# Latent attention of a two-block layer stack: a TensorE step begins with its scores, and each item's transposes stand ahead of another item's values

## The reference, cut to what matters

```
sc = jnp.einsum('bqhd,bkhd->bhqk', qi, k, preferred_element_type=jnp.float32) * scale
mask = key_chunk[None, :] <= q_chunk[:, None]
p = jax.nn.softmax(jnp.where(mask, sc, -jnp.inf), axis=-1)
return jnp.einsum('bhqk,bkhd->bqhd', p.astype(v.dtype), v)
```

## Time and profile before

| | us |
|---|---|
| median of 3 runs (2577.3 to 2577.61) | 2577.58 |
| the profiled execution | 2577.62 |
| its span in the trace | 2575.8 |
| PE busy in the span | 2557.3 |
| DVE busy | 1662.4 |
| ACT busy | 1276.7 |
| POOL busy | 360.7 |

### The profile page before, as it was taken

The page is one execution under the profiler, slowest core; times in us unless marked ns, Lnnn a source line. Parts: engine busy times, 40 slices in busy tenths (PEclk is TensorE's granted clock), DMA queues, the critical chain, the costliest instruction groups (busy, mean ns, idle before and its releaser), DMA issues.

```text
span 2575.8 us, 35285 instructions
## 1 busy us (share of the span) xinstructions
PE 2557.3 (99%) x12630; PEld 2030.0 (79%) x12630; DVE 1662.4 (65%) x2398; ACT 1276.7 (50%) x2142; POOL 360.7 (14%) x270
## 2 busy tenths in 40 slices
PE   9999999999999999999999999999999999999999
PEld 7855788888777557888888775799988777899887
DVE  4476677643988895677653778597633546687533
ACT  4326543333546895444333578577533425567432
POOL 0020100000103782100000130000610002000800
PEclk9999999999999999999999999999999999999999
DMA  5330232223243442233222230232232221232222
GB/s 216 106 94 21 91 107 97 92 97 98 82 133 123 131 131 81 72 109 98 96 93 96 95 103 10 65 116 101 89 112 93 96 97 51 97 123 99 82 98 98
DMA packets 74833, 250.44 MB, mean 97 GB/s; under 512 B 8764, under 2 KB 9148, under 8 KB 74336
## 3 DMA queue, kind: packets, MB, share of 16 engines
q1 hardware_dynamic: 73632, 240.63, 28.5%
q0 software_dynamic: 944, 8.33, 0.9%
q10 hardware_dynamic: 144, 0.00, 0.0%
HBM read 242.50 MB, written 2.24 MB: 95 GB/s over the span
## 4 chain that ended last, share of the span: by engine, by line
PE 92%; DVE 3%; ACT 2%; issue 1%; DMA 1%; SPq 0%; POOL 0%; DVEq 0%; ACTq 0%; POOLq 0%
PE bank L432 25%; PE bank L433 24%; PE bank L434 24%; PE bank L1361 2%; PE bank L1363 2%; PE bank L1362 2%; PE bank L2257 2%; PE bank L2808 1%; PE bank L654 1%; PE bank L639 1%; PE bank L3156 1%; PE bank L1706 1%; PE bank L640 1%; PE bank L1695 1%; PE bank L2264 1%
## 5 line engine op out<-in xcount | busy, mean ns | idle before, releaser
L383 DVE TENSOR_TENSOR wlo<-wraw,whi 128x1024 fp32r<-128x1024 f32 x344 | 441.5, 1285 | 448.8 <-ACT whi L360 448.2
L360 ACT ACTIVATE whi<-wraw 128x1024 fp32r<-128x1024 f32 x348 | 366.9, 1056 | 508.5 <-DMA wraw<-in_w 508.3
L432 PE MATMUL bank<-hnhi,whi 128*128 128x512 f32 (+1 forms) x1528 | 596.7, 390 | 1.1 <-DVE wlo L383 0.7
L433 PE MATMUL bank<-hnlo,whi 128*128 128x512 f32 (+1 forms) x1528 | 584.5, 383 | 0.0
L434 PE MATMUL bank<-hnhi,wlo 128*128 128x512 f32 x1392 | 542.1, 389 | 0.0
L432 PE MATMUL bank<-ahi,whi 128*128 128x512 f32 x1184 | 463.5, 391 | 1.9 <-DVE alo L712 1.1
L434 PE MATMUL bank<-ahi,wlo 128*128 128x512 f32 x1184 | 460.8, 389 | 0.0
L433 PE MATMUL bank<-alo,whi 128*128 128x512 f32 x1184 | 460.8, 389 | 0.0
L432 PEld LDWEIGHTS bank<-hnhi,whi 128*128 128x128 f32 x1528 | 287.2, 188 | 86.3 <-issue 29.5
L433 PEld LDWEIGHTS bank<-hnlo,whi 128*128 128x128 f32 x1528 | 287.4, 188 | 57.5 <-issue 3.4
L434 PEld LDWEIGHTS bank<-hnhi,wlo 128*128 128x128 f32 x1392 | 261.3, 188 | 55.7
(11 more groups left out here) (360 smaller groups left out, 3940.5 us busy)
## 6 DMA issues: line engine op xcount, KB each, us to landing
wraw<-in_w SPq DMA_DIRECT2D x410, 512.0 KB, 3.3
arena<-cs_scratch SPq DMA_DIRECT2D x20, 512.0 KB, 5.9
over_a<-cs_scratch SPq DMA_DIRECT2D x12, 512.0 KB, 6.1
arena<-in_rpb POOLq DMA_DIRECT2D x1, 2880.0 KB, 14.1
arena<-in_t_step POOLq DMA_DIRECT2D x2, 897.0 KB, 5.1
mT<-arena SPq DMA_DIRECT2D x28, 64.0 KB, 2.0
out_dram<-xT SPq DMA_DIRECT2D x7, 256.0 KB, 2.0
arena<-in_t_ab POOLq DMA_DIRECT2D x1, 1472.0 KB, 6.7
```

Of the source, the lines that this page charges most:

```text
L360: act.activation(whi[:, slot * BLOCK:(slot + 1) * BLOCK], wraw[:, slot * BLOCK:(slot + 1) * BLOCK], ACT.Copy).then_inc(sem("w_hi"), 1)
L383: dve.tensor_tensor(low_home(i), wraw[:, slot * BLOCK:(slot + 1) * BLOCK], whi[:, slot * BLOCK:(slot + 1) * BLOCK], ALU.subtract).then_inc ...
L432: pe.matmul(out, wh, ah, start=start, stop=False)
L433: pe.matmul(out, wh, al, start=False, stop=False)
```

## The change

Two blocks of `pe_mla_step` change places with their neighbours. In a step s the scores of the step now stand ahead of the transposes of item 2s - 4, where they stood behind them. And the values of item 2s - 5 now stand between the transposes of item 2s - 4 and those of item 2s - 3, where they stood behind both. The waits of every piece go with it. Nothing else changes: the lists of DVE, ACT, POOL and SP are the same.

```diff
-            if 2 <= s <= 17:
-                turn(2 * s - 4)
             if s < 16:
                 scores(s)
+            if 2 <= s <= 17:
+                turn(2 * s - 4)
             for j, lo, hi in {16: ((0, 0, 2),), 17: ((0, 2, 4),), 18: ((1, 2, 4),)}.get(s, ()):
                 pe_row(pe, "mla_o", j, lo, hi)
+            if s >= 3:
+                values(2 * s - 5)
             if 2 <= s <= 17:
                 turn(2 * s - 3)
-            if s >= 3:
-                values(2 * s - 5)
             if s == 17:
                 pe_row(pe, "mla_o", 1, 0, 2)
             if 2 <= s <= 17:
                 values(2 * s - 4)
```

More of the change, by code:

```diff
@@ L2845, in values @@
                 mm.then_inc(sem("item_valued"), 1)
+            if s < 16:
+                scores(s)
             if 2 <= s <= 17:
                 turn(2 * s - 4)
-            if s < 16:
-                scores(s)
             for j, lo, hi in {16: ((0, 0, 2),), 17: ((0, 2, 4),), 18: ((1, 2, 4),)}.get(s, ()):
                 pe_row(pe, "mla_o", j, lo, hi)
+            if s >= 3:
+                values(2 * s - 5)
             if 2 <= s <= 17:
                 turn(2 * s - 3)
-            if s >= 3:
-                values(2 * s - 5)
             if s == 17:
```

## The result

The changed kernel takes 2621.17 us (median of 4 runs, 2619.36 to 2623.35) against 2577.48 before (4 runs, 2577.30 to 2577.61). The ratio is 1.0171, with a 95% interval of 1.0159 to 1.0184: 43.7 us or 1.7% slower. The forecast was 2611.5 us, slower, in a range of 2602 to 2623. So direction and range held, and the forecast was 9.7 us short: it had 33.9 us of the loss of 43.7.

What follows compares the result with a forecast made beforehand. PE was taken to bound the kernel, busy 2557.3 of 2575.8 us. Thirteen rounds totalling 97.7 us plus 5.8 at the end make 103.5 against 69.6: 2577.6 + 33.9 = 2611.5 us, range 2602 to 2623.

Steps and rivals of the forecast that it cites:

- the stretch: Latent attention, from the end of step 2's scores (1551.24) to step 16's first output product: 69.6 us before, 103.5 forecast.
- a ring: Latent attention: scores, turn (transposes), copy, exponentials, normalisation, two maxima, next scores' second half, all in one line; 7.5 us each time.
- The price of a round: One pass from a step's scores to the next step's: 4.74 us plus amounts growing with item width; 13 total 97.7 us.
- the four slopes: Added per width step k (0 to 3): turn and copy 0.44, exponentials and normalisation 0.345, maxima 0.535, scores 0.39 us.
- The tail of 5.8: After the last scores: turn and copy 1.65, exponentials and normalisation 2.74, maxima 1.41 us, before the first output product.
- small pieces in the ring: Odd items' copies, exponentials, normalisations, small splits and collections: taken as nothing, up to 0.5 us a round, 6.5 in all.
- nothing is given back behind: Behind step 16: PE has the same work in nearly the same order, all ready, so no time is regained.
- The second half of the edit: Values ahead of the second turn: hidden behind ACT and DVE, PE's part 3.2 us at most against 4.2; cost nothing.
- the sum: Latent attention: 97.7 plus 5.8 makes 103.5 us where 69.6 stood, so + 33.9 us.
- the first rival: PE's clock falls to half throughout the latent attention: + 29.3 us more, 2641 us; chance 0.08.
- PE's busy time unchanged near 66: Sign: from 1551.24 to step 16's first L432, PE's busy time stays near 66 us while the span grows to about 103.5.
- PE waits of 30 us or more at L2808: Sign: PE's score matmuls wait for the maxima, some 2 us a step at the even item, 30 us or more total.

Runs made afterwards that it cites:

- two thirds filled kernel: The changed kernel with extra identity matmuls ending steps 2 to 14, about two thirds of a first count that overran: 2612.53 us, ratio 1.0138.

## Why the prediction was right, and where it fell short

- *PE bounds, with 3.0 us idle in the stretch.* Right. No kernel tried here is measurably faster; turning the order of ACT round in the kernel before gives 0.9998.
- *The change closes a ring; none of its stations needs the one before, but each engine's order holds it.* Shown. Turning round one order on ACT or one on DVE removes 37 or 34 of some 44 us; lengthening a link adds 6.95 us to eleven rounds where 6.99 was forecast; lengthening a neighbour by as much adds 0.01 to them.
- *The price of a round, 4.74 us and the four slopes.* Right to 0.1 us in rounds at full clock (7.41 and 7.33, 7.45 and 7.38, and eleven rounds of the two thirds filled kernel). Over all 13 rounds of that kernel it is 99.2 us for 97.7: 0.6 us in the eleven at full clock, 0.9 in the two that are not. The tail of 5.8 was 5.91 at full clock. So the 6.5 us a side that the range allowed for small pieces in the ring and for quicker handing over were hardly used. (The forecast less 6.5 is 2605.0, not 2604.) All of it came from the trace of before, as start-to-start distances.
- *The start isn't moved, nothing is given back behind.* Right: 1551.24 in both, and 955.6 us behind for 955.0.
- *The second half of the edit costs nothing.* Right in this kernel, wrong by itself: 3.5 us, since PE fits the split values less tightly.
- *What fell short is the clock, which the sum put at nothing.* The sum held it at 1.00, the upper bound allowed some for "a clock that dips in a few rounds" (2623 is 5.0 us above what the uncosted pieces give), and its full fall had a chance of 0.08. What happened lies between: 0.86 on average over the stretch, below 1.00 in nine of 13 rounds and in the tail. In time, the filling took 6.6 us off the stretch (112.39 to 105.79); its two rounds and its tail below 1.00 hold another 0.9 and 0.7. That is 8.2 us, a little over a quarter of the first rival's 29. With the sum's 33.9, the 0.6 of the rounds and the 0.1 of the tail it makes the 42.8 us by which the stretch grew. By the medians the filling gave 8.6 us, or 8.1 when each kernel is held against its own runs of the kernel before. So the result lies in the range, 1.8 us under its upper end, by the allowance and not by the sum.
- "PE's busy time unchanged near 66" failed with it: it is 83.2, since records at the lower clock are longer. Not all of the 16.7 us more lie on the ring.
- The page of the Trainium skill cited there, "TensorE: Matmul & The Clock Gate", section "HAM oscillation — how this bites in real kernels", had the direction: a PE that pauses between groups of matmuls lost clock, again and again. The page tells it of pauses in which PE waits for a DMA; here PE waited for DVE's maxima, at most 3.0 us at a time. The row that I set against it, busy 73% at a clock of 1.00, could not answer: the changed stretch is busy 83.22 of 112.39 us, 74%, and reads 0.86.
- *PE waits of 30 us or more at L2808.* It was 23.0, with up to 3.0 in one. That slower matmuls fill part of the gaps is likely, but not shown.
- *A step of 7 to 8.6 us, the longest being the one that ends with step 6.* The rounds took 7.41 to 8.90, and step 4's is the longest, at a clock of 0.83. Among those at 1.00 step 6's is the longest, 8.76.

Left open: why the clock stayed at 1.00 in some rounds and fell in others. Rounds 9 and 14 have gaps as well. With the values not between the turns (2622.87 against 2621.17) the difference is within the two intervals. In that kernel the rounds that end with steps 6, 9 and 13 read 1.00 as well and are as long to the last digit (8.76, 7.45, 7.45), so the values between the turns give nothing back there; its stretch, 115.31 us, reads 0.79.

## What to carry to other kernels

Where several engines pass items round by hand-written orders, a moved block can close a ring without any data needing it. Write down, for each engine, what stands ahead of what, follow one item's successor all the way round, and add up start-to-start distances; the loss is that sum less the step of today, times the steps. Do it for every order that is turned round, also for the one that looks harmless. And when a change opens gaps on a PE that had none, price the clock as a partial loss on top of the sum, not as a rare other case.

## What the runs showed that I had not expected

- Extra matmuls that compute nothing made the kernel faster: 2621.2 us without, 2612.5 with 81 more, 2616.4 with 117. The granted clock rose from 0.86 in the stretch to 0.95 and 1.00, and the eight score records of step 3 went from 3.54 us to 2.19 and 1.99.
- The same 268 value records took 17.7 us of PE in one group a step and 20.6 in two, at nearly the same length of a record (278 and 283 ns): splitting a step's values in two costs PE about 0.2 us (2.9 us over the 13 steps of the stretch that have two groups).
